# LRU gate products on 64 rows of TensorE, two at a time in two banks, with the second tile of outputs first

## The chip, the cores and the metric

The kernel runs on one core of one Trainium2 chip. The metric is the device time of one execution in microseconds (us). The kernel before takes 2714.79 us (median of 3 runs, 2714.78 to 2714.88).

## The reference

A decoder trunk of two layers on x of 1024 tokens by 1024 channels, in float32: layer 0 mixes tokens by retention, layer 1 by a Griffin block (below), each followed by a SwiGLU FFN, and one last norm. The change touches only the gates of the Griffin block, whose width is 1536 in 8 blocks of 192 channels:

```python
gate, u = jnp.split(h @ w_in, 2, axis=-1)
u = conv4(u) + conv_b
ub = u.reshape(B, S, LRU_BLOCKS, LRU_BLOCK_W)
r = sigmoid(einsum('bsnc,ncd->bsnd', ub, w_r) + b_r)
i = sigmoid(einsum('bsnc,ncd->bsnd', ub, w_i) + b_i)
log_a = (-LRU_C * softplus(-lam)) * r
a = exp(log_a)
b = sqrt(-expm1(2.0 * log_a)) * (i * u)
hs = scan(a, b)                      # hs[t] = a[t] * hs[t-1] + b[t]
y = hs * gelu(gate)
return y @ w_out
```

## The kernel before

**Products.** Each float32 matrix is kept as two fp32r parts, hi and lo. One product of a 128x128 weight tile with 512 tokens is three matmuls of TensorE, written by `three` (L745): hi by hi (L747), hi of the weights by lo (L750), lo of the weights by hi (L751). They add up in one bank of PSUM. PSUM has eight banks of 512 columns, and every output that a bank holds is an event: event e lies in bank e mod 8. TensorE raises the semaphore `psum_full` when an event is complete; the reader raises `psum_free` when it has used it. `free(e)` (L742) lets TensorE begin event e only when event e-8 and all before it have been read.

**Groups.** The 1536 channels are worked in four groups of 384, which is 2 blocks of 192 or 3 tiles of 128. Group g runs on TensorE in this order: `lru_into` for u (3 tiles), `lru_into` for the gelu gate (3 tiles), `lru_outof` (L1250) of the group before, then `lru_gates` (L1232). After the gates come the first tile of the next group's `lru_into`, which begins with `free` on its second event (L781), or in the last group four output blocks of the group before, each with a `free` of its own (L1282). Groups 0 and 3 are written out (L1257 to L1259, L1268 to L1290); groups 1 and 2 are a loop (L1260).

**The gates.** For each half of the tokens (hf) and each tile of outputs, r and i (m_i) are each one event. Blocks of 192 do not fall on tiles of 128. Outputs of tile 0 need input tiles 0 and 1, those of tile 1 need 0, 1 and 2, those of tile 2 need 1 and 2 (`MEETS`, L52). Of input tile 1 only rows 0 to 63 matter for output tile 0, and only rows 64 to 127 for output tile 2; the other 64 rows of those weight tiles (`wri_hi`, `wri_lo`) are zeros. A half of a group is 2 x (2 + 3 + 2) products, 42 matmuls, and a group 84.

**What the gates feed.** ScalarE (`gate_chain`, L1736) and VectorE (`gate_chain`, L2353) take items 0 to 5 in the order of the events: item i is tile i mod 3 of half i // 3. For one item ScalarE computes the sigmoid of r (L1743) and of i (L1748), then, two items together, tanh (L1757), exp (L1761) and sqrt (L1767), each behind a load of its table. VectorE multiplies u by i (L2361, `gated`; this raises `psum_free` by 2 for the item's two events), then L2369, L2373, the scan L2378 and the product with gelu (L2385). The order around the change, on ScalarE and on VectorE:

```python
gates(0); gates(1); tanh_exp((0, 1)); roots((0, 1)); gates(2); gates(3); y_round((0, 1))
gated((0, 1)); scans((0, 1), amid=lambda: gated((2,))); gated((3,)); y_split((0, 1)); gated((4, 5))
```

`amid` runs behind the first scan of a pair. L2390 (`y_split`) raises `y_ready`, for which `lru_outof` and the last output products (L1298) wait.

**u.** The conv writes `uc`; ScalarE rounds it to hi (L1733) and VectorE subtracts for lo (L2351, raises `u_ready`), in four pieces: tile 0, tile 1, and tile 2 in two halves. In groups 1 and 2 the hi and lo parts share their memory with those that `lru_outof` reads, so tile 2's pieces are made only when `lru_outof` is through. VectorE adds the outputs of `lru_outof` to the residual with L1952.

Of the kernel before, what the change touches and what calls it, by code (L numbers as in the profile page):

```python
# [14 lines left out]
P = 128  # L15
D = 1024
S = 1024
# [9 lines left out]
GT = 3  # L27
# [21 lines left out]

OT_AT = (0, SCORE_AT[3])  # L50

MEETS = [(0, 1), (0, 1, 2), (1, 2)]  # L52

U_PIECES = [(0, 0, S), (1, 0, S), (2, 0, BANK), (2, BANK, S)]

# [108 lines left out]
def build(nc, x, positions, mix_norm, ffn_norm, final_norm, ret_w_in, ret_w_out, lru_w_in, lru_conv_w,  # L164
# [3 lines left out]
    with ctx:  # L168
# [572 lines left out]
        def _(pe):  # L741
# [490 lines left out]
            def lru_gates(g, base, e0, u_hi, u_lo):  # L1232

                pe.wait_ge(wri_ready, 2 * g + 2)
                for hf in range(2):
                    for tile in range(GT):
                        for m_i in range(2):
                            e = e0 + (hf * GT + tile) * 2 + m_i
                            free(base + e)
                            if m_i == 0 and (hf, tile) in ((0, 0), (0, 1), (1, 1)):  # L1240

                                pe.wait_ge(u_ready, len(U_PIECES) * g + 2 + tile + hf)
                            for kt in MEETS[tile]:
                                w = slice(m_i * 1152 + kt * 384 + tile * P, m_i * 1152 + kt * 384 + (tile + 1) * P)
                                r = slice(kt * S + hf * 512, kt * S + (hf + 1) * 512)
                                m = three(bank(e), wri_hi[:, w], wri_lo[:, w], u_hi[:, r], u_lo[:, r],
                                          kt == MEETS[tile][0], kt == MEETS[tile][-1])
# [25 lines left out]
            for first in (0, 4):  # L1273
                for k in range(GT):
                    if first == 0:
                        pe.wait_ge(y_ready, (GROUPS - 2) * 6 + k + 4)
                        pe.wait_ge(w_ready, u0 + 12 + k + 1)
                    w = slice(k * 512, (k + 1) * 512)
                    for s in range(first, first + 4):
                        e = (L_OUT if first == 0 else L_OUT_LAST - 4) + s  # L1280
                        if k == 0:
                            free(base + e)  # L1282
                        c = k * S + s * P
                        m = three(bank(e), a_hi[:, c:c + P], a_lo[:, c:c + P], w_hi[:, w], w_lo[:, w],
                                  k == 0, k == GT - 1, s == (4 if k else 0))
                        if k == GT - 1:
                            m.then_inc(psum_full, 1)
                if first == 0:
                    lru_gates(GROUPS - 1, base, L_RI_LAST, h_hi, h_lo)
# [5 lines left out]

            def y_there(half, k, i):
                if i == 0:
                    pe.wait_ge(y_ready, (GROUPS - 1) * 6 + half * GT + k + 1)  # L1298
                if half == 0 and k == 0:

                    pe.wait_ge(psum_free, by_halves(3, 0, i) - 8 + 1)
# [9 lines left out]
        def _(act):  # L1311
# [424 lines left out]
            def gate_chain(g, base, e0, y_hi):  # L1736
                def gates(i):

                    tile = i % GT
                    if i >= 4:  # L1740
                        act.wait_ge(l_scan, 6 * g + i - 3)
                    full(base + e0 + 2 * i)
# [8 lines left out]
                def tanh_exp(items):  # L1751

                    for i in items:
                        if i >= 2:
                            act.wait_ge(l_scan, 6 * g + i - 1)
                        act.wait_ge(r_sig, 6 * g + i + 1)
                        nc.scalar.activation(s_buf[i % 2], r_buf[i % 4], ACT.Tanh,  # L1757
                                             scale=gc_gate[:, 21 + i % GT:22 + i % GT]).then_inc(r_tanh, 1)
                    for i in items:
                        act.wait_ge(r_tanh, 6 * g + i + 1)  # L1760
                        nc.scalar.activation(r_buf[i % 4], r_buf[i % 4], ACT.Exp,  # L1761
                                             scale=gc_gate[:, i % GT:i % GT + 1]).then_inc(a_exp, 1)

                def roots(items):

# [3 lines left out]
                def y_round(items):  # L1769
                    for i in items:  # L1770
                        act.wait_ge(y_out, 6 * g + i + 1)

                        act.wait_ge(psum_full, base + e0 + (6 if i < GT else 12))
                        at = i % GT * S + i // GT * 512
# [48 lines left out]
        def _(dve):  # L1823
# [528 lines left out]

            def gate_chain(g, y_hi, y_lo, meanwhile=lambda nh, blocks: None):  # L2353
                def cut(i):
                    return slice(i % GT * S + i // GT * 512, i % GT * S + i // GT * 512 + 512)

                def gated(items):

# [4 lines left out]
                def scans(items, between=lambda: None, amid=lambda: None):  # L2363
# [9 lines left out]
                        step.up(TT(uc[:, cut(i)], uc[:, cut(i)], s_buf[i % 2], ALU.mult))  # L2373
                    for j, i in enumerate(items):
                        dve.wait_ge(dve_step, first + j + 3)
                        tile, hf = i % GT, i // GT
# [121 lines left out]
```

## Time and profile before

| | before |
|---|---|
| median of 3 runs | 2714.79 us |
| the profiled execution's own time | 2714.54 us |
| its span | 2712.7 us |
| TensorE busy | 2673.3 us, 99% |
| VectorE busy | 1274.1 us, 47% |
| ScalarE busy | 826.6 us, 30% |
| GpSimd busy | 1259.5 us, 46% |
| mean granted TensorE clock | 0.998 |
| chain that ended last: TensorE, VectorE, ScalarE | 92%, 4%, 2% |

The span is the time from the first to the last instruction that the profiler saw; the time of an execution has 1.8 us more around it. Busy matmuls overlap each other, since a matmul's duration is counted to the end of its results. So the distance between the starts of two matmuls, and not their duration, is what one costs on TensorE.

### The profile page before, as it was taken

The numbers are of one execution on the slowest core, as the hardware profiler recorded it, in microseconds if no ns is written. First come the engines' busy times: TensorE is split into PE (matmuls) and PEld (weight loads), VectorE is DVE, ScalarE is ACT, GpSimd is POOL, SyncE is SP. The second block draws the span as 40 slices with busy tenths as digits, with TensorE's granted clock in tenths as the row PEclk, the third lists the DMA queues.
The fourth block names the chain that finished last, engine by engine and source line by source line (L and its number), as shares of the span: only waits on it lengthen the run. The fifth ranks groups of instructions, "written<-read, shape, count | busy, mean of one in ns | idle before, by whom it ended". The sixth has DMA issues, their size and how long they took to land.

```text
span 2712.7 us, 35233 instructions
## 1 busy us (share of the span) xinstructions
PE 2673.3 (99%) x12017; PEld 2212.2 (82%) x12017; DVE 1274.1 (47%) x1730; ACT 826.6 (30%) x1384; POOL 1259.5 (46%) x1204
## 2 busy tenths in 40 slices
PE   8999999999999999999999999999999999999998
PEld 6888888888888788888888788888877888888886
DVE  8333322323335854444444537365587444444445
ACT  3120120120124533333323524334355222222224
POOL 4324323323423466655555445363454556555553
PEclk9999999999999999999999999999999999999999
DMA  4101101101111111111211011111111111111212
GB/s 142 43 28 63 43 31 60 46 32 59 47 36 43 51 51 54 46 46 54 63 53 54 28 55 44 36 59 36 44 55 47 55 54 46 46 51 54 66 50 82
DMA packets 173624, 139.29 MB, mean 51 GB/s; under 512 B 9184, under 2 KB 143456, under 8 KB 173536
## 3 DMA queue, kind: packets, MB, share of 16 engines
q1 hardware_dynamic: 171440, 133.46, 15.8%
q10 hardware_dynamic: 2096, 4.62, 0.5%
q8 instruction: 59, 0.97, 0.1%
q14 instruction: 29, 0.24, 0.0%
HBM read 132.81 MB, written 5.24 MB: 51 GB/s over the span
## 4 chain that ended last, share of the span: by engine, by line
PE 92%; DVE 4%; ACT 2%; issue 1%; DMA 0%; POOL 0%; SPq 0%; DVEq 0%; ACTq 0%
PE ps L747 30%; PE ps L750 30%; PE ps L751 30%; DVE f_h_lo L2104 1%; PE ps L983 0%; ACT gate_buf L1318 0%; DVE residual L2289 0%; DVE residual L2451 0%; PE ps L823 0%; DVE h_sum_a L2093 0%; DVE gate_buf L2178 0%; DVE residual L1952 0%; DMA residual<-in_x 0%; ACT f_h_hi L1556 0%; DVE f_h_lo L2093 0%
## 5 line engine op out<-in xcount | busy, mean ns | idle before, releaser
L587 POOL TENSOR_TENSOR f_w_lo<-f_raw,f_w_hi 128x512 fp32r<-128x512 f32 x270 | 357.6, 1326 | 448.5 <-ACT f_w_hi L1507 366.0
L747 PE MATMUL ps<-f_h_hi,f_w_hi 128*128 128x512 f32 x1232 | 481.1, 391 | 4.9 <-DVE f_h_lo L2104 2.1
L751 PE MATMUL ps<-f_h_hi,f_w_lo 128*128 128x512 f32 x1232 | 479.5, 389 | 0.0
L750 PE MATMUL ps<-f_h_lo,f_w_hi 128*128 128x512 f32 x1232 | 479.4, 389 | 0.0
L545 POOL TENSOR_TENSOR small<-w_raw 128x1 f32<-128x1 f32 x200 | 59.9, 300 | 805.7 <-PE ps L747 796.1
L2289 DVE TENSOR_TENSOR residual<-ps,residual 128x512 f32<-128x512 f32 x352 | 239.3, 691 | 172.5 <-PE ps L751 172.5
L747 PEld LDWEIGHTS ps<-f_h_hi,f_w_hi 128*128 128x128 f32 x1232 | 231.2, 188 | 58.9 <-issue 4.3
L1507 ACT ACTIVATE f_w_hi<-f_raw 128x512 fp32r<-128x512 f32 x246 | 154.6, 629 | 384.0 <-PE ps L751 383.9
L751 PEld LDWEIGHTS ps<-f_h_hi,f_w_lo 128*128 128x128 f32 x1232 | 231.2, 188 | 48.3
L750 PEld LDWEIGHTS ps<-f_h_lo,f_w_hi 128*128 128x128 f32 x1232 | 231.3, 188 | 47.1
L747 PE MATMUL ps<-f_w_hi,f_act_hi 128*128 128x512 f32 x688 | 267.9, 389 | 0.6 <-POOL f_w_lo L587 0.6
L750 PE MATMUL ps<-f_w_lo,f_act_hi 128*128 128x512 f32 x688 | 267.6, 389 | 0.0
L751 PE MATMUL ps<-f_w_hi,f_act_lo 128*128 128x512 f32 x688 | 267.6, 389 | 0.0
L556 POOL TENSOR_TENSOR w_lo<-w_raw,w_hi 128x512 fp32r<-128x512 f32 x190 | 259.1, 1364 | 15.2
L747 PE MATMUL ps<-h_hi,w_hi 128*128 128x512 f32 x632 | 247.4, 392 | 0.1
L751 PE MATMUL ps<-h_hi,w_lo 128*128 128x512 f32 x632 | 246.0, 389 | 0.0
L750 PE MATMUL ps<-h_lo,w_hi 128*128 128x512 f32 x632 | 245.9, 389 | 0.0
L587 POOL TENSOR_TENSOR f_w_lo<-f_sum,f_w_hi 128x512 fp32r<-128x512 f32 x124 | 178.7, 1441 | 132.0 <-ACT f_w_hi L1507 124.6
L747 PE MATMUL ps<-w_hi,h_hi 128*128 128x512 f32 x528 | 205.7, 390 | 0.3 <-DVE gate_buf L1975 0.3
L751 PE MATMUL ps<-w_hi,h_lo 128*128 128x512 f32 x528 | 205.5, 389 | 0.0
L750 PE MATMUL ps<-w_lo,h_hi 128*128 128x512 f32 x528 | 205.5, 389 | 0.0
L2244 DVE TENSOR_TENSOR gate_buf<-ps,gate_buf 128x512 f32<-128x512 f32 x120 | 82.7, 689 | 235.2 <-PE ps L751 235.1
(302 smaller groups left out, 4630.3 us busy)
## 6 DMA issues: line engine op xcount, KB each, us to landing
f_raw<-in_ffn_w_gu SPq DMA_DIRECT2D x176, 256.0 KB, 3.3
w_raw<-in_ret_w_in SPq DMA_DIRECT2D x96, 256.0 KB, 2.7
f_raw<-in_ffn_w_down SPq DMA_DIRECT2D x88, 256.0 KB, 2.7
w_raw<-in_lru_w_in SPq DMA_DIRECT2D x48, 256.0 KB, 2.9
w_raw<-in_ret_w_out SPq DMA_DIRECT2D x32, 256.0 KB, 2.5
w_raw<-in_lru_w_out SPq DMA_DIRECT2D x24, 256.0 KB, 2.6
residual<-in_x SPq DMA_DIRECT2D x8, 512.0 KB, 7.1
out_y<-residual SPq DMA_DIRECT2D x8, 512.0 KB, 2.6
```

Source lines behind the costliest of these rows:

```text
L545: nc.gpsimd.tensor_tensor(small[:, 62:63], col, col, ALU.subtract)
L556: nc.gpsimd.tensor_tensor(lo, raw[:, cut], hi.bitcast(F32), ALU.subtract).then_inc(w_ready, 1)
L587: nc.gpsimd.tensor_tensor(lo, src, hi.bitcast(F32), ALU.subtract).then_inc(f_wready, 1)
L747: m = nc.tensor.matmul(o, l_hi, r_hi, start=start, stop=False, skip_group_check=onto)
L750: nc.tensor.matmul(o, l_hi, r_lo, start=False, stop=False, skip_group_check=onto)
L751: return nc.tensor.matmul(o, l_lo, r_hi, start=False, stop=stop, skip_group_check=onto)
L1507: nc.scalar.activation(f_unit(j, last)[0], src, ACT.Copy).then_inc(f_whi, 1)
L2104: TT(H_lo[:, h_cut(form, k)], src[:, t_cut(k)], H_hi[:, h_cut(form, k)].bitcast(F32), ALU.subtract).then_inc(hn_dve, 1)
L2244: TT(t, f_bank(u, p), t, ALU.add).then_inc(f_ev, 1)
L2289: TT(X[:, c], ps[:, b * BANK:(b + 1) * BANK], X[:, c], ALU.add).then_inc(f_ev, 1)
```

## The change

The gates' products are issued in another order, and those that meet only half of the rows are cut to these rows. For each half of the tokens TensorE now issues: output tile 0 by input tile 0 (r and i), output tile 1 by input tiles 0, 1 and 2, output tile 2 by input tile 2, and last (`halves_meet`) output tile 0 by rows 0 to 63 of input tile 1, alternating with output tile 2 by rows 64 to 127 of it. The two lie in two banks. Matmuls stay 42 per half: 30 of 128 rows and 12 of 64 rows. The events, and with them ScalarE's and VectorE's items, go by `GATE_TILES`: items 0 and 3 are tile 1, 1 and 4 tile 0, 2 and 5 tile 2. Items of tiles 0 and 2 are announced together, by one increment of 4 on the last matmul. The waits for `u_ready`, `psum_free` and `y_ready` move with that.

```diff
-MEETS = [(0, 1), (0, 1, 2), (1, 2)]
+GATE_TILES = (1, 0, 2)
...
                 for hf in range(2):
-                    for tile in range(GT):
+                    def event(tile, m_i):
+                        return e0 + (hf * GT + GATE_TILES.index(tile)) * 2 + m_i
+
+                    def operands(tile, m_i, kt, rows=slice(0, P)):
+                        w = slice(m_i * 1152 + kt * 384 + tile * P, m_i * 1152 + kt * 384 + (tile + 1) * P)
+                        r = slice(kt * S + hf * 512, kt * S + (hf + 1) * 512)
+                        return wri_hi[rows, w], wri_lo[rows, w], u_hi[rows, r], u_lo[rows, r]
+
+                    def meets(tile, kt, start, stop):
                         for m_i in range(2):
-                            e = e0 + (hf * GT + tile) * 2 + m_i
-                            free(base + e)
-                            if m_i == 0 and (hf, tile) in ((0, 0), (0, 1), (1, 1)):
-
-                                pe.wait_ge(u_ready, len(U_PIECES) * g + 2 + tile + hf)
-                            for kt in MEETS[tile]:
...
-                            m.then_inc(psum_full, 1)
+                            e = event(tile, m_i)
+                            if start:
+                                free(base + e)
+                            m = three(bank(e), *operands(tile, m_i, kt), start, stop)
+                            if stop:
+                                m.then_inc(psum_full, 1)
+
+                    def halves_meet():
+
+                        for m_i in range(2):
+                            a_w, a_wl, a_u, a_ul = operands(0, m_i, 1, slice(0, 64))
+                            b_w, b_wl, b_u, b_ul = operands(2, m_i, 1, slice(64, P))
+                            a, b = bank(event(0, m_i)), bank(event(2, m_i))
+                            nc.tensor.matmul(a, a_w, a_u, start=False, stop=False)
+                            nc.tensor.matmul(b, b_w, b_u, start=False, stop=False)
+                            nc.tensor.matmul(a, a_w, a_ul, start=False, stop=False)
+                            nc.tensor.matmul(b, b_w, b_ul, start=False, stop=False)
+                            nc.tensor.matmul(a, a_wl, a_u, start=False, stop=True)
+                            m = nc.tensor.matmul(b, b_wl, b_u, start=False, stop=True)
+
+                        m.then_inc(psum_full, 4)
+
+                    if hf == 0:
+                        pe.wait_ge(u_ready, len(U_PIECES) * g + 2)
+                    meets(0, 0, True, False)
+                    meets(1, 0, True, False)
+                    meets(1, 1, False, False)
+                    pe.wait_ge(u_ready, len(U_PIECES) * g + 3 + hf)
+                    meets(1, 2, False, True)
+                    meets(2, 2, True, False)
+                    halves_meet()
...
-                        pe.wait_ge(y_ready, g * 6 + k + 4)
+                        pe.wait_ge(y_ready, g * 6 + GATE_TILES.index(k) + 4)
...
-                    tile = i % GT
+                    tile = GATE_TILES[i % GT]
```

The other lines of the diff put `GATE_TILES` in the place of `i % GT` or of `k` wherever an item or an output product names its tile.

TensorE at the start of the gates of group 0 (`wri` are the gates' weights, `a` is u; the change shifts the line numbers, so L747 is now L749). Before:

```order
L747 MATMUL ps<-a_hi,wri_hi 128x512 [waits u_ready,psum_free,wri_ready]
L750 MATMUL ps<-a_lo,wri_hi 128x512
L751 MATMUL ps<-a_hi,wri_lo 128x512
L747 MATMUL ps<-a_hi,wri_hi 128x512
L750 MATMUL ps<-a_lo,wri_hi 128x512
L751 MATMUL ps<-a_hi,wri_lo 128x512
L747 MATMUL ps<-a_hi,wri_hi 128x512 [waits psum_free]
```

and now:

```order
L749 MATMUL ps<-a_hi,wri_hi 128x512 [waits psum_free,u_ready,wri_ready]
L752 MATMUL ps<-a_lo,wri_hi 128x512
L753 MATMUL ps<-a_hi,wri_lo 128x512
L749 MATMUL ps<-a_hi,wri_hi 128x512 [waits psum_free]
L752 MATMUL ps<-a_lo,wri_hi 128x512
L753 MATMUL ps<-a_hi,wri_lo 128x512
L749 MATMUL ps<-a_hi,wri_hi 128x512 [waits psum_free]
```

The first two events that TensorE opens are those of item 1 (tile 0), each with one product of three matmuls; item 0 (tile 1) is opened behind them. In order of issue the matmul that completes item 0's r is now the 21st and was the 6th, and item 1's r and i are complete with the 42nd and were with the 21st and the 30th.

TensorE at the end of the first half of the tokens, same group, before:

```order
L751 MATMUL ps<-a_hi,wri_lo 128x512
L747 MATMUL ps<-a_hi,wri_hi 128x512 [waits psum_free]
L750 MATMUL ps<-a_lo,wri_hi 128x512
L751 MATMUL ps<-a_hi,wri_lo 128x512
L747 MATMUL ps<-a_hi,wri_hi 128x512
```

and now:

```order
L753 MATMUL ps<-a_hi,wri_lo 128x512
L1261 MATMUL ps<-a_hi,wri_hi 128x512
L1262 MATMUL ps<-a_hi,wri_hi 128x512
L1263 MATMUL ps<-a_lo,wri_hi 128x512
L1264 MATMUL ps<-a_lo,wri_hi 128x512
L1265 MATMUL ps<-a_hi,wri_lo 128x512
L1266 MATMUL ps<-a_hi,wri_lo 128x512
L1261 MATMUL ps<-a_hi,wri_hi 128x512
```

L1261, L1263 and L1265 read rows 0 to 63, the other three rows 64 to 127; the six stand there twice, for r and for i.

TensorE from the last matmul of group 0's gates to the next group, now (before, the same rows stand there with their own lines, and the wait too):

```order
L1266 MATMUL ps<-a_hi,wri_lo 128x512
L1290 UNCONDITIONAL_BRANCH
L1290 ISA
L757 ISA [waits psum_free]
L749 MATMUL ps<-h_hi,w_hi 128x512 [waits w_ready]
L752 MATMUL ps<-h_lo,w_hi 128x512
```

The wait at L757 (L755 before) is `free` on the next group's second event, which is fulfilled when item 2 has been read by `gated`. Nothing moves there, and neither on ScalarE nor on VectorE: their rows are the same in number and order, with other tiles in them.

## Rows read from the trace of the kernel before

**Rows 1.** The page's part 1: busy time, share of the span and instructions
```profile
PE 2673.3 (99%) x12017; PEld 2212.2 (82%) x12017; DVE 1274.1 (47%) x1730; ACT 826.6 (30%) x1384; POOL 1259.5 (46%) x1204
```

**Rows 2.** Waits of TensorE, 1550 to 2100 us: total, times, longest us
```profile
PE ps L747 <- DVE a_lo L2351: 1.6, 2, 0.8
...
PE ps L747 <- DVE uc L2361: 0.2, 1, 0.2
```

**Rows 3.** Matmuls that read the gates' weights: count, ns min/median/max, starts
```profile
L747 PE MATMUL ps<-a_hi,wri_hi x84: 389/389/496, 1623.5 to 1878.0; 128*128 128x512 f32 x84
...
L747 PE MATMUL ps<-h_hi,wri_hi x28: 389/389/389, 1952.1 to 1970.5; 128*128 128x512 f32 x28
```

**Rows 4.** Timeline of TensorE, group 0's gates: start us, duration us, what
```profile
1623.53 0.39 PE L747 MATMUL ps<-a_hi,wri_hi 128*128 128x512 f32 x1
1623.53 0.19 PEld L750 LDWEIGHTS ps<-a_lo,wri_hi 128*128 128x128 f32 x1
1623.76 0.39 PE L750 MATMUL ps<-a_lo,wri_hi 128*128 128x512 f32 x1
...
1642.57 0.39 PE L747 MATMUL ps<-h_hi,w_hi 128*128 128x512 f32 x1
```

**Rows 5.** Timeline of ScalarE and VectorE, group 0
```profile
1630.53 0.69 ACT L1748 ACTIVATE xn<-ps,gc_gate 128x512 f32<-128x512 f32 x1 [1.35 <-PE ps L751]
...
1640.69 0.67 DVE L2361 TENSOR_TENSOR uc<-uc,xn 128x512 f32<-128x512 f32 x1
```

**Rows 6.** Chain of waits, 1950 to 1980 us (group 3): start us, us, what
```profile
1959.12 0.69 ACT xn L1748
...
1972.27 0.61 DVE uc L2361
1972.92 0.50 PE ps L747
```

**Rows 7.** Timeline, group 1's gates, of TensorE, ScalarE and VectorE
```profile
1740.49 0.39 PE L747 MATMUL ps<-a_hi,wri_hi 128*128 128x512 f32 x1
...
1744.15 0.50 PE L747 MATMUL ps<-a_hi,wri_hi 128*128 128x512 f32 x1 [0.78 <-DVE a_lo L2351]
...
1748.59 0.69 ACT L1748 ACTIVATE xn<-ps,gc_gate 128x512 f32<-128x512 f32 x1 [0.35 <-PE ps L751]
...
1758.75 0.66 DVE L2361 TENSOR_TENSOR uc<-uc,xn 128x512 f32<-128x512 f32 x1
...
1760.62 0.39 PE L747 MATMUL ps<-h_hi,w_hi 128*128 128x512 f32 x1
```

**Rows 8.** Timeline of TensorE: starts of gates 2 and 3, end of 2
```profile
1858.54 0.39 PE L747 MATMUL ps<-a_hi,wri_hi 128*128 128x512 f32 x1
...
1878.68 0.39 PE L747 MATMUL ps<-h_hi,w_hi 128*128 128x512 f32 x1
...
1952.12 0.39 PE L747 MATMUL ps<-h_hi,wri_hi 128*128 128x512 f32 x1
```

**Rows 9.** Timeline of VectorE: residual adds ahead of group 1's gates
```profile
1738.64 4.86 DVE L1952 TENSOR_TENSOR residual<-ps,residual 128x512 f32<-128x512 f32 x8
```

**Rows 10.** Timeline of weight loads in a run of matmuls of 128 columns
```profile
324.18 0.19 PEld L751 LDWEIGHTS ps<-a_hi,a_lo 128*128 128x128 f32 x1
...
324.29 0.19 PEld L747 LDWEIGHTS ps<-a_hi 128*128 128x128 f32 x1
```

**Rows 11.** TensorE's wait before layer 1, and windows (third number from the end: granted clock)
```profile
1548.42 5.09 PE L885 MATMUL ps<-ident,xn 128*128 128x128 f32 x24 [2.92 <-DVE xn L1849]
...
1545.00:1550.00 5.00, 2.00 (x8) 0.80 (x7) 3.66 (x9) 4.23 (x10) 0.00 (x0) 0.90 0.01 2
1550.00:1555.00 5.00, 5.00 (x29) 4.70 (x30) 3.97 (x8) 4.62 (x8) 1.10 (x2) 0.76 0.00 0
```

**Rows 12.** Timeline: last `y_split` on VectorE, and the output products that need it
```profile
2007.59 1.47 DVE L2390 TENSOR_TENSOR h_lo<-gate_buf,h_hi 128x512 fp32r<-128x512 f32 x2
...
2012.54 0.39 PE L747 MATMUL ps<-w_hi,h_hi 128*128 128x512 f32 x1
```

More of the change, by code:

```diff
@@ L1235, in lru_gates @@
                 for hf in range(2):
-                    for tile in range(GT):
-                        for m_i in range(2):
-                            e = e0 + (hf * GT + tile) * 2 + m_i
-                            free(base + e)
-                            if m_i == 0 and (hf, tile) in ((0, 0), (0, 1), (1, 1)):
-                                pe.wait_ge(u_ready, len(U_PIECES) * g + 2 + tile + hf)
-                            for kt in MEETS[tile]:
[L1244 to L1247, printed above, removed]
-                            m.then_inc(psum_full, 1)
+                    def event(tile, m_i):
+                        return e0 + (hf * GT + GATE_TILES.index(tile)) * 2 + m_i
@@ L1275, in _ @@
                     if first == 0:
-                        pe.wait_ge(y_ready, (GROUPS - 2) * 6 + k + 4)
+                        pe.wait_ge(y_ready, (GROUPS - 2) * 6 + GATE_TILES.index(k) + 4)
                         pe.wait_ge(w_ready, u0 + 12 + k + 1)
@@ L1297, in y_there @@
                 if i == 0:
-                    pe.wait_ge(y_ready, (GROUPS - 1) * 6 + half * GT + k + 1)
+                    pe.wait_ge(y_ready, (GROUPS - 1) * 6 + half * GT + GATE_TILES.index(k) + 1)
                 if half == 0 and k == 0:
@@ L1757, in tanh_exp @@
                         nc.scalar.activation(s_buf[i % 2], r_buf[i % 4], ACT.Tanh,
-                                             scale=gc_gate[:, 21 + i % GT:22 + i % GT]).then_inc(r_tanh, 1)
+                                             scale=gc_gate[:, 21 + GATE_TILES[i % GT]:22 + GATE_TILES[i % GT]])\
+                            .then_inc(r_tanh, 1)
                     for i in items:
@@ L1761, in tanh_exp @@
                         nc.scalar.activation(r_buf[i % 4], r_buf[i % 4], ACT.Exp,
-                                             scale=gc_gate[:, i % GT:i % GT + 1]).then_inc(a_exp, 1)
+                                             scale=gc_gate[:, GATE_TILES[i % GT]:GATE_TILES[i % GT] + 1])\
+                            .then_inc(a_exp, 1)
                 def roots(items):
@@ L1773, in y_round @@
                         act.wait_ge(psum_full, base + e0 + (6 if i < GT else 12))
-                        at = i % GT * S + i // GT * 512
+                        at = GATE_TILES[i % GT] * S + i // GT * 512
                         nc.scalar.activation(y_hi[:, at:at + 512], R3[:, at:at + 512], ACT.Copy)\
@@ L2354, in cut @@
                 def cut(i):
-                    return slice(i % GT * S + i // GT * 512, i % GT * S + i // GT * 512 + 512)
+                    at = GATE_TILES[i % GT] * S + i // GT * 512
+                    return slice(at, at + 512)
                 def gated(items):
@@ L2375, in scans @@
                         dve.wait_ge(dve_step, first + j + 3)
-                        tile, hf = i % GT, i // GT
+                        tile, hf = GATE_TILES[i % GT], i // GT
                         start = uc[:, tile * S + 511:tile * S + 512] if hf else 0.0
```

## The prediction

> **What bounds the kernel now.** I read the page's busy shares first: TensorE is busy for 2673.3 of 2712.7 us, 99%, and no other engine for half of the span [rows 1]. So a microsecond of TensorE's work counts if nothing else keeps TensorE waiting at that place, and a wait put in front of TensorE counts in full. Next, the waits of TensorE in layer 1 [rows 2]. Two belong to the change. One is for u's lo part (L2351), twice 0.8 us. The other is for `gated` (L2361), 0.2 us: short, but it tells that the gate chain of ScalarE and VectorE is already level with TensorE at one place. That is what decides here.
>
> The cost of a matmul is the distance of starts. 4 x 84 matmuls read the gates' weights (84 + 28 of each of the three forms) [rows 3]. Group 0's 84 take from 1623.53 to 1642.57 us, when the next group's first one starts: 19.04 us, or 0.2267 us each, which I call a slot. A matmul lasts 0.39 us until its results are there, 0.16 us longer than its slot, and the weights of the next are loaded meanwhile, in 0.19 us [rows 4].
>
> **The chain behind the gates.** I count from T0, the start of a group's first gate matmul. In group 0 the sigmoid of item 1's i starts at T0 + 7.00 (1630.53), 0.04 us behind the result of the 30th matmul (T0 + 29 slots + 0.39 = T0 + 6.96). Item 2 has been read at 1640.69 + 0.67 = 1641.36, T0 + 17.83 [rows 5]. That is 10.83 us from the one to the other. The distance repeats where I look: 1748.59 to 1759.41 in group 1 [rows 7]. It holds tanh, exp and sqrt of two items with their table loads, and four operations and a scan of VectorE, all in a row; their order does not change. In group 0 the next group can begin at T0 + 17.9 and TensorE comes at T0 + 19.04: the chain has 1.1 us to spare. In group 3 it has none: the chain of waits runs from the sigmoid at 1959.12 (T0 + 7.00 again, T0 being 1952.12 [rows 8]) to `gated` of item 3 and from there into the matmul at 1972.92 [rows 6].
>
> **1. Item 1 is complete later.** It was complete with the 30th matmul, r long before i; now both come with the last of the first half. If two half-row matmuls share a slot, that is the last of 30 + 6 slots: its result is there at T0 + 35 slots + 0.39 = T0 + 8.32. The second of a pair needs its own load; where loads follow each other as closely as they can, their starts are 0.11 us apart [rows 10], so I add 0.11. Sigmoid of r at T0 + 8.48; the one of i, which waited alone before, comes some 0.58 us behind it (a ScalarE operation of this size, 0.69 us less the overlap of 0.11), at T0 + 9.06. The chain is 2.06 us later, plus what the entry into 64-row matmuls costs, d.
>
> **2. The entry, d.** No row shows a change from 128 to 64 rows. Below: 0, the load hides as in every row. A gain is excluded, since the half-row matmuls move the same 512 columns and two loads fill 0.22 of a 0.227 us slot. Above: the results before must be out (0.16 us) and the load is bare (0.19 us), 0.35 us [rows 4]. I take 0.2, between the ends but nearer the bare drain. The Trainium skill, "TensorEngine Tiling (Array Packing)", Key Properties, says that a change of tiling mode drains TensorE; no run here shows it yet, and by it d would lie between 0.16 and 0.35, which leaves the result as it is.
>
> **3. The next start of TensorE, group by group.** Item 2 read at T0 + 17.83 + 2.06 + d = T0 + 19.89 + d; the matmul follows 0.05 us later [rows 6], and a restart costs 0.15 us in the matmuls behind it. This is from group 1: its 84 take 20.13 us, of which the wait itself is 0.94 (1744.15 against T0 + 12 slots = 1743.21) and 0.15 the rest [rows 7]. So T0 + 20.1 + d in every group.
> - Group 0: 19.04 before, so +1.06 + d.
> - Groups 1 and 2: 20.13 and 20.14 before [rows 7, 8], since they waited for tile 2's u after 12 matmuls. Now this wait stands behind 18 matmuls, T0 + 4.08, and u was there at T0 + 3.6: it vanishes. The new place comes out the same: -0.03 and -0.04, + d each.
> - Group 3: behind its gates four output blocks begin, the third of which needs item 3. It began at T0 + 20.80 [rows 6, 8] and now 2.06 + d later.
>
> **4. Earlier events at the start.** TensorE now opens item 1's events first, which lie two banks further. In groups 1 and 2 this asks that the third residual add be through: adds start 0.6 us apart from 1738.64, so it ends at 1740.52, against T0 = 1740.49 [rows 9, 7]. With the restart 0.2 us in each, 0.4.
>
> **5. What TensorE saves.** Twelve slots a group, 48 x 0.2267 = 10.9 us, and the 2.2 us of the u waits. It is ready for the next group at T0 + 16.3, plus up to 1.4 us for going into and out of 64 rows twice, so at T0 + 17.7 at the latest, and waits until T0 + 20.3. All of it becomes waiting, and the second half's entry is hidden there too. The cover is the chain; without it, TensorE's time would count.
>
> **6. Other waits.** `y_ready` of the last group is given at 2009.06 and the products that need its items start at 2012.54 [rows 12]; both shift with TensorE. Nothing in the work of the DMA queues, ScalarE or VectorE is added.
>
> Sum: 1.06 - 0.03 - 0.04 + 2.06 + 0.4 + 4 x 0.2 = 4.25 us; 3.45 with d = 0 and 4.85 with d = 0.35. Against the profiled execution's 2714.54 this gives 2718.8; the median of the runs is 0.25 higher, so 2719.0.
>
> The Trainium skill ("Trainium Kernel Development and Optimization", Best Practices) warns of this change as such: tiling TensorE speeds up the products but not what empties PSUM. The group 3 wait agrees (0.2 us for `gated` already). Counted by TensorE alone, the sum would be the gain of rival C below.
>
> **Rivals.** A measurement of this kernel can tell about 0.2%, 5.4 us, from no change.
> - **A, the forecast**: pairs share slots, the chain sets the next start. 2718.2 to 2719.6. Chance 0.62; in 0.05 of it an unseen cost lifts it above the bound, as more than 0.5 us of d a group would.
> - **B, slower: the half-row matmuls do not run side by side.** Place: `halves_meet` of the first half. The change then only reorders. Each pair takes two slots, the chain starts 6 slots - 0.11 = 1.25 us later in each of four groups, +5.0: 2724.0. It decides from the point where a pair takes over 0.28 us (0.05 us more for each of the 24 pairs on the chain is 1.2 us). For it: nothing in the trace has ever run two matmuls at once, and loads need 0.11 us each, so that a pair's two loads just fit in a slot. Against: the two have different rows and banks, and the load rate does suffice. 0.15. The Trainium skill ("TensorE: Matmul & The Clock Gate", Part 3) says that matmuls on different row groups overlap; no row here shows it, and by it B would be out.
> - **D, slower: TensorE's clock falls in the new waits.** TensorE would now stand still for some 2.6 us in each group (its last result at T0 + 16.5 + 0.2 for the seconds of the pairs + 4 x 0.2 = T0 + 17.5, the restart at T0 + 20.1 + d). The trace has one wait of that size in full swing: 2.92 us at 1545.5, followed by short transposes. The granted clock is then 0.90 and 0.76 over two windows of 5 us, part of the time at 1.2 instead of 2.4 GHz: (0.10 + 0.24) x 5 = 1.7 us lost [rows 11]. Against: those transposes leave TensorE's array mostly unused, here full matmuls follow at once. Two falls give +3.4: 2722.4; one 2720.7, four 2725.8. Chance 0.18.
> - **C, faster: TensorE's own work counts**, because the chain is shorter than I read. Minus 10.9, minus 2.2, plus 8 x 0.4 for entries and exits: -9.9, 2704.9. Against it stand the 10.83 us that repeat and the wait for `gated` that is there now. 0.05.
>
> **The numbers.** A is the likeliest, so 2719.0. Within 0.2% lies most of A: 0.57. Slower: B, D and the rest of A, 0.15 + 0.18 + 0.05 = 0.38. Faster: C, 0.05. The range begins a little under A's lower end, 2717.4, for steps of the chain that I may have counted 0.2 us too long in each group, and reaches over one or two falls of the clock to B with d = 0.3, 2724.4. It leaves out C and the worst of D.
>
> **What will show it.** In the changed kernel the sigmoid of item 1's i should start about 9.3 us behind the first gate matmul, and be followed by `gated` of item 2 after 10.8 us. TensorE should show three or four new waits for `gated`, some 2 to 3 us each, and none for tile 2's u; starts from first gate matmul to next group 20.3 us in groups 0 to 2. In `halves_meet` the starts of the two matmuls of a pair should lie 0.11 us or less apart and pairs 0.23 us; 0.23 us from each to the next is B. A granted clock under 1.00 behind the gates is D. I am wrong in the main if TensorE does not wait for `gated`, or if item 2's release moves by another amount than item 1.

## The result, and the profile after

The change takes 2724.08 us (median of 6 runs, 2723.8 to 2725.94) against 2714.89 for the kernel before on the same chip (6 runs, 2714.78 to 2717.12): ratio 1.0034, 95% interval 1.0024 to 1.0044. It is slower by 9.2 us, 0.34%, which is beyond the 0.2% that the prediction took for no change. The forecast was 2719.0; the time lies at the upper end of the range. What lies between is rival D, not with one or two falls of the clock but with all four.

The page's part 1 of the changed kernel, against [rows 1]:

```profile
PE 2672.5 (98%) x12017; PEld 2206.3 (81%) x12017; DVE 1277.0 (47%) x1730; ACT 826.0 (30%) x1384; POOL 1258.4 (46%) x1204
```

TensorE's busy time moves by 0.8 us, although 48 slots of 0.227 us are gone: this line shows neither what was saved nor what was lost. The loss is in the waits of TensorE, 1550 to 2100 us (total, times, longest):

```profile
PE ps L749 <- DVE uc L2394: 12.1, 5, 3.0
```

It was 0.2 us in one wait [rows 2], and the row for u's lo part is gone. Timeline of TensorE, the pairs of group 0's first half:

```profile
1630.54 0.39 PE L753 MATMUL ps<-a_hi,wri_lo 128*128 128x512 f32 x1
1630.86 0.49 PE L1261 MATMUL ps<-a_hi,wri_hi 64*128 64x512 f32 x1
1630.86 0.49 PE L1262 MATMUL ps<-a_hi,wri_hi 64*128 64x512 f32 x1
1631.19 0.39 PE L1263 MATMUL ps<-a_lo,wri_hi 64*128 64x512 f32 x1
1631.20 0.39 PE L1264 MATMUL ps<-a_lo,wri_hi 64*128 64x512 f32 x1
...
1632.45 0.50 PE L749 MATMUL ps<-a_hi,wri_hi 128*128 128x512 f32 x1
1632.79 0.40 PE L752 MATMUL ps<-a_lo,wri_hi 128*128 128x512 f32 x1
```

The two of a pair start together and take one slot. Going in costs 0.09 us (0.32 from 1630.54 to 1630.86, against 0.23) and 0.10 in the next distance; coming out costs about as much again. From 1630.54 to 1632.79, eight distances of starts, it is 2.25 us in place of 1.81, so once in and once out costs 0.44. The chain behind it, timelines of ScalarE, VectorE and TensorE in group 0, whose T0 is now 1623.97:

```profile
1633.15 0.68 ACT L1778 ACTIVATE xn<-ps,gc_gate 128x512 f32<-128x512 f32 x1
...
1643.30 0.67 DVE L2394 TENSOR_TENSOR uc<-uc,xn 128x512 f32<-128x512 f32 x1
...
1644.10 0.49 PE L749 MATMUL ps<-h_hi,w_hi 128*128 128x512 f32 x1 [2.97 <-DVE uc L2394]
```

Item 1's i is at T0 + 9.18 (T0 + 7.00 before, [rows 5]), item 2 has been read 10.82 us later (10.83), and the next group starts at T0 + 20.13 (19.04, [rows 4]) behind a wait of 2.97 us. The other groups, same timeline, of each T0 and the next start, and in group 3 the third output block too:

```profile
1743.82 0.50 PE L749 MATMUL ps<-a_hi,wri_hi 128*128 128x512 f32 x1
...
1764.10 0.49 PE L749 MATMUL ps<-h_hi,w_hi 128*128 128x512 f32 x1 [2.97 <-DVE uc L2394]
...
1863.81 0.50 PE L749 MATMUL ps<-a_hi,wri_hi 128*128 128x512 f32 x1
...
1884.03 0.69 PE L749 MATMUL ps<-h_hi,w_hi 128*128 128x512 f32 x1 [2.89 <-DVE uc L2394]
...
1959.21 0.39 PE L749 MATMUL ps<-h_hi,wri_hi 128*128 128x512 f32 x1
...
1979.26 0.50 PE L749 MATMUL ps<-w_hi,a_hi 128*128 128x512 f32 x1 [2.89 <-DVE uc L2394]
...
1982.18 0.79 PE L749 MATMUL ps<-w_hi,a_hi 128*128 128x512 f32 x1 [0.39 <-DVE uc L2394]
```

Behind each of the four waits stand matmuls of another speed. Timeline behind the first, and windows around the first three (the number before the last two is the granted clock):

```profile
1645.43 0.63 PE L753 MATMUL ps<-h_hi,w_lo 128*128 128x512 f32 x1
1645.85 0.63 PE L749 MATMUL ps<-h_hi,w_hi 128*128 128x512 f32 x1
...
1648.41 0.51 PE L749 MATMUL ps<-h_hi,w_hi 128*128 128x512 f32 x1
```

```profile
1640.00:1645.00 5.00, 2.03 (x14) 1.34 (x11) 5.00 (x7) 3.87 (x6) 0.27 (x1) 1.00 0.00 0
1645.00:1650.00 5.00, 5.00 (x17) 3.96 (x16) 4.63 (x8) 4.29 (x8) 4.92 (x3) 0.66 0.00 0
1760.00:1765.00 5.00, 2.03 (x13) 1.32 (x10) 5.00 (x7) 3.87 (x6) 0.27 (x1) 0.97 0.00 0
1765.00:1770.00 5.00, 5.00 (x17) 3.97 (x16) 4.63 (x8) 4.29 (x8) 4.92 (x3) 0.69 0.00 0
1880.00:1885.00 5.00, 2.11 (x13) 1.35 (x12) 5.00 (x7) 3.88 (x6) 0.13 (x1) 0.92 0.02 3
1885.00:1890.00 5.00, 5.00 (x18) 4.00 (x17) 4.63 (x8) 4.27 (x8) 4.92 (x3) 0.74 0.00 0
```

For some 3 us a matmul costs 0.42 us in place of 0.227: 1.2 GHz in place of 2.4. Each pair of windows lacks 0.34 x 5 = 1.7 us. From the next group's start to the following T0 it is 99.72, 99.71 and 75.18 us, where it was 97.92, 97.92 and 73.44.

The account, up to the start of layer 1's FFN, where both kernels wait for the same add (before, then after):

```profile
2034.58 0.50 PE L747 MATMUL ps<-f_h_hi,f_w_hi 128*128 128x512 f32 x1 [1.48 <-DVE residual L1952]
```

```profile
2044.26 0.50 PE L749 MATMUL ps<-f_h_hi,f_w_hi 128*128 128x512 f32 x1 [1.45 <-DVE residual L1984]
```

That is 9.68 us: 0.44 was there at T0 of group 0; the starts behind the gates give 1.09 + 0.15 + 0.08 + 2.17 = 3.49; the stretches between them 1.80 + 1.79 + 1.74; the last one, 1982.18 to 2044.26 against 1972.92 to 2034.58, 0.42.

### The profile page after: what moved, and what is told of

Its sections match the earlier page's. It is cut to its first block, busy times and chain, and to the rows that moved or that the text cites. A ratio compares the mean times of both kernels' runs of the same rounds, so it can differ in the third digit from the quotient of the medians.

```text
span 2722.4 us, 35229 instructions
## 1 busy us (share of the span) xinstructions
PE 2672.5 (98%) x12017; PEld 2206.3 (81%) x12017; DVE 1277.0 (47%) x1730; ACT 826.0 (30%) x1384; POOL 1258.4 (46%) x1204
## 4 chain that ended last, share of the span: by engine, by line
PE 92%; DVE 4%; ACT 3%; issue 1%; DMA 0%; POOL 0%; SPq 0%; DVEq 0%; ACTq 0%
PE ps L749 30%; PE ps L753 30%; PE ps L752 30%; DVE f_h_lo L2136 1%; PE ps L985 0%; ACT gate_buf L1348 0%; DVE residual L2321 0%; DVE residual L2484 0%; PE ps L825 0%; DVE h_sum_a L2125 0%; PE ps L887 0%; DVE gate_buf L2210 0%; DMA residual<-in_x 0%; ACT f_h_hi L1586 0%; DVE f_h_lo L2125 0%
## 5 line engine op out<-in xcount | busy, mean ns | idle before, releaser
L749 PE MATMUL ps<-f_h_hi,f_w_hi 128*128 128x512 f32 x1232 | 481.1, 391 | 4.8 <-DVE f_h_lo L2136 2.1
L547 POOL TENSOR_TENSOR small<-w_raw 128x1 f32<-128x1 f32 x200 | 51.8, 259 | 816.0 <-PE ps L749 806.1
L749 PEld LDWEIGHTS ps<-f_h_hi,f_w_hi 128*128 128x128 f32 x1232 | 231.2, 188 | 59.0 <-issue 4.4
L749 PE MATMUL ps<-f_w_hi,f_act_hi 128*128 128x512 f32 x688 | 267.9, 389 | 0.6 <-POOL f_w_lo L589 0.6
L749 PE MATMUL ps<-h_hi,w_hi 128*128 128x512 f32 x632 | 249.9, 395 | 8.8 <-DVE uc L2394 8.8
L749 PE MATMUL ps<-w_hi,h_hi 128*128 128x512 f32 x528 | 205.7, 390 | 0.3 <-DVE gate_buf L2007 0.3
```

The costliest lines, as they stand in the source:

```text
L547: nc.gpsimd.tensor_tensor(small[:, 62:63], col, col, ALU.subtract)
L749: m = nc.tensor.matmul(o, l_hi, r_hi, start=start, stop=False, skip_group_check=onto)
```

## The experiments

Each ran beside the kernel before on the same chip, in 5 rounds. That one's medians there were 2715.46 us for experiments 1, 2, 4 and 5, 2715.08 for 6, 7 and 10, and 2714.79 for 3, 8 and 9. The change itself did not run again beside them, so differences to it of less than 1 us say nothing. In the expectations T1 is the account above (the chain and the clock), called the first theory here; T2 and T3 are rivals to it. Falls and waits are read from one execution of each kernel, the profiled one.

**1. Are the half rows what counts?** The change with all 128 rows in the pairs, so that nothing can run side by side:

```diff
-a_w, a_wl, a_u, a_ul = operands(0, m_i, 1, slice(0, 64))
-b_w, b_wl, b_u, b_ul = operands(2, m_i, 1, slice(64, P))
+a_w, a_wl, a_u, a_ul = operands(0, m_i, 1)
+b_w, b_wl, b_u, b_ul = operands(2, m_i, 1)
```

> The change with its order, but the 12 half-row matmuls of each half read all 128 rows (the other 64 rows of those weights are zeros), so nothing can share a slot. Chain theory (T1: the next start is set by the release of item 2, and the clock falls because TensorE stands still for 3 us): item 1's sigmoid of i starts at T0 + 10.3 instead of 9.2, the next group at T0 + 21.3; TensorE is ready at T0 + 19.04 and stands for about 2.1 us. If that is too short for the clock to fall, 2722.7 us, a little below the change though it has 48 slots more on TensorE; if it falls in all four, 2728.5. Rival T2 (the fall of the clock comes from the 64-row matmuls, not from standing still): granted clock 1.00 behind the gates, 2722.7. Rival T3 (pairs cost or save something on the path): the time would differ from the change by the 10.9 us of the 48 slots, 2735.

Measured: 2725.36 us, ratio 1.0035 (1.0021 to 1.0049). It lies between the two times of the first theory. In the profiled execution, the slowest of the five (2727.78 us), the clock fell behind two of the four waits and not behind the others; the other four took 2724.77 to 2725.38 us at a mean granted clock of 0.997 and 0.998 in place of 0.996, so they had fewer falls. Timeline of TensorE, three of the starts:

```profile
1645.87 0.49 PE L749 MATMUL ps<-h_hi,w_hi 128*128 128x512 f32 x1 [2.06 <-DVE uc L2394]
...
1767.01 0.49 PE L749 MATMUL ps<-h_hi,w_hi 128*128 128x512 f32 x1 [2.05 <-DVE uc L2394]
...
1981.17 0.50 PE L749 MATMUL ps<-w_hi,a_hi 128*128 128x512 f32 x1 [1.98 <-DVE uc L2394]
```

and the windows behind these three:

```profile
1645.00:1650.00 5.00, 4.13 (x13) 3.32 (x14) 4.88 (x9) 3.18 (x7) 3.49 (x2) 0.74 0.00 0
...
1770.00:1775.00 5.00, 5.00 (x24) 4.14 (x23) 3.36 (x4) 4.97 (x8) 4.84 (x5) 1.00 0.07 17
...
1980.00:1985.00 5.00, 3.27 (x8) 2.16 (x9) 5.00 (x8) 3.18 (x6) 0.00 (x0) 0.69 0.00 0
1985.00:1990.00 5.00, 5.00 (x16) 3.88 (x16) 1.63 (x3) 4.97 (x8) 2.04 (x3) 0.63 0.00 0
```

48 slots more of TensorE's work, 10.9 us, cost 1.3 us by the medians, and 0.7 when each kernel is compared with its own runs of the kernel before. In the profiled executions the stretch from T0 of group 0 to the FFN's first matmul is 423.22 us, against 420.29: the first halves' pairs make the chain later by 1.1 us in each group, 4.5 together, and the clock takes 1.5 less. The second halves' 24 slots end in the wait and cost nothing. Behind waits of the same 2.0 us the clock fell or did not, so executions can differ in this; behind the last one it stayed low for twice as long.

**2. The same waits, filled.** The change with 12 matmuls by weights that are zeros (added onto a sum that is still open, so nothing changes in it) ahead of the pairs of each group's second half:

```diff
                     meets(2, 2, True, False)
+                    if hf == 1:
+                        for _ in range(4):
+                            z, r = slice(256, 384), slice(512, 1024)
+                            three(bank(event(2, 0)), wri_hi[:, z], wri_lo[:, z], u_hi[:, r], u_lo[:, r], False, False)
                     halves_meet()
```

> The change, with 12 more matmuls of 128 rows (zero weights, 2.7 us) per group ahead of the second half's pairs, so that TensorE works where it stood still. T1: the chain is untouched, the next group starts at T0 + 20.1 as in the change, TensorE stands 0.3 us instead of 3.0 there, the granted clock stays at 1.00, and the kernel gets about 5.8 us faster than the change, 2718.3, by 48 matmuls more. T2 (64-row matmuls lower the clock): 2724, as the change, clock still falls. If TensorE's own work counted: 2724 + 10.9 = 2735.

Measured: 2718.95 us, ratio 1.0014 (1.0005 to 1.0023), 5.1 us under the change. Waits of TensorE:

```profile
PE ps L749 <- DVE uc L2398: 2.1, 5, 1.3
```

The next groups start at T0 + 20.13, 20.29, 20.23 and 20.06, as in the change, and the granted clock is 1.00 in every window around them. More work on the busiest engine made the kernel faster than the change is.

**3. Half the fill** (`range(2)` in place of `range(4)`), to see a length in between.

> e2_fill_wait with 6 in place of 12 fill matmuls a group: the waits for `gated` should be 1.36 us longer than there, 1.5 to 1.6 us in groups 0 to 3, and the starts of the next groups the same, T0 + 20.1 to 20.3. The question is TensorE's clock: behind waits of 3.0 us it fell in four of four, behind 2.0 us in two of four, behind 1.3 us in none. If it falls behind none, the time is that of e2_fill_wait, 2719 us; each fall adds about 1.45 to 1.8 us; four would give 2725.

Measured: 2719.16 us, ratio 1.0015 (1.0006 to 1.0024). Waits of TensorE, and windows behind the first two:

```profile
PE ps L749 <- DVE uc L2398: 7.5, 5, 1.6
```

```profile
1645.00:1650.00 5.00, 5.00 (x24) 4.13 (x23) 4.64 (x8) 3.84 (x7) 4.74 (x3) 1.00 0.01 3
...
1765.00:1770.00 5.00, 5.00 (x24) 4.13 (x23) 4.22 (x6) 4.98 (x9) 4.92 (x4) 1.00 0.00 0
```

The same chain, the same starts, 5.4 us more waiting than in 2, and the time of 2. So waiting itself costs nothing here while the clock stays, and the 64-row matmuls by themselves do not lower it; the whole 4.9 us to the change are the falls. They can be read piece by piece: from a group's end to the next T0 this kernel takes 98.10, 98.15 and 73.58 us. The change takes 1.62, 1.56 and 1.60 more, and 0.46 more at the end: 5.2 together in the profiled executions.

**4. Sooner for item 1.** `GATE_TILES` (0, 1, 2) again, pairs kept: tile 0 by input 0, the pairs (which open tile 2's banks), tile 1, then tile 2 by input 2. `meets` and `halves_meet` take m_i here, and each event is announced by itself:

```diff
-                    meets(0, 0, True, False)
-                    meets(1, 0, True, False)
-                    meets(1, 1, False, False)
-                    pe.wait_ge(u_ready, len(U_PIECES) * g + 3 + hf)
-                    meets(1, 2, False, True)
-                    meets(2, 2, True, False)
-                    halves_meet()
+                    for m_i in range(2):
+                        meets(0, m_i, 0, True, False)
+                    for m_i in range(2):
+                        halves_meet(m_i)
+                    for m_i in range(2):
+                        meets(1, m_i, 0, True, False)
+                        meets(1, m_i, 1, False, False)
+                        if m_i == 0:
+                            pe.wait_ge(u_ready, len(U_PIECES) * g + 3 + hf)
+                        meets(1, m_i, 2, False, True)
+                    for m_i in range(2):
+                        meets(2, m_i, 2, False, True)
```

> The pairs without the new order: items are tiles 0, 1, 2 as before; TensorE issues tile 0 by input 0, then the pairs (tile 2 is opened by them), then tile 1, then tile 2 by input 2. Item 0 complete at 12 matmuls and item 1 at 30, as before, plus 0.32 us for going into and out of 64 rows. T1: item 1's sigmoid of i at T0 + 7.3, next start at T0 + 18.35 in group 0 (19.04 before), 1.3 us sooner than before in groups 1 and 2 (tile 2's u is no longer waited for, but 0.5 us for a residual add is), 0.3 us later in group 3; TensorE stands for 1.3 us and the clock stays at 1.00: 2711.8. T2 (64-row matmuls lower the clock): 4 x 1.45 us more, 2717.6, with a granted clock under 1.00 behind the gates. If TensorE's own work counted: 2705.

Measured: 2712.15 us, ratio 0.9988 (0.9979 to 0.9997), as the first theory had it. Starts at T0 + 18.42, 18.59, 18.50 and 18.34, behind waits of 1.0 to 1.2 us, no fall. It is 3.3 us under the kernel before. The two waits for u that are gone (1.09 us each with their restarts) make up 2.2 of it; what the pairs alone bring in this order no run shows.

**5. Item 2 released from the chain.** The change, with item 2's sigmoids ahead of tanh on ScalarE (`gates(2)` before `tanh_exp((0, 1))`) and on VectorE `gated((0, 1, 2))` in place of `amid`.

> The change, with ScalarE's sigmoids of item 2 and VectorE's product with them moved ahead of tanh of items 0 and 1, so that item 2's banks are read some 9 us sooner. T1: TensorE no longer waits for item 2 in groups 0 to 2 and begins the next group at T0 + 17.0 with a clock of 1.00; the chain of items 0 to 5 ends about 0.6 us later than in the change, so a wait of about 1.4 us for the conv of the next group appears instead before its second gate tile; in group 3 item 3 is read at T0 + 23.5, TensorE stands 5 us there and the clock falls once. Sum about +0.6 us against before: 2715.4, between 2713 and 2718. If the release of item 2 does not set the next start: 2724, as the change.

Measured: 2729.07 us, ratio 1.0051 (1.0038 to 1.0065). Missed by 13.7 us. Timelines of TensorE, VectorE and GpSimd:

```profile
1640.65 0.50 PE L749 MATMUL ps<-h_hi,w_hi 128*128 128x512 f32 x1
...
1642.94 1.62 POOL L558 TENSOR_TENSOR w_lo<-w_raw,w_hi 128x512 fp32r<-128x512 f32 x1
1643.33 2.31 DVE L2411 TENSOR_TENSOR_SCAN uc<-tmp,uc 128x512 f32<-128x512 f32 x1
...
1688.12 0.49 PE L749 MATMUL ps<-h_hi,w_hi 128*128 128x512 f32 x1 [3.66 <-DVE uc L2368]
...
1986.13 0.79 PE L749 MATMUL ps<-w_hi,a_hi 128*128 128x512 f32 x1 [4.79 <-DVE uc L2394]
```

The first step came true: the next group starts at T0 + 17.09, with no wait. But the same chain has a second end, the next group's conv, for which TensorE now stands still for 3.66 us at 1688.12 (1.4 reckoned). ScalarE's two operations moved into it make it 1.1 us longer. And TensorE, 3 us earlier, gives GpSimd its weights 3 us earlier: GpSimd's first operation behind the gates starts at 1641.29 and not at 1644.73, and VectorE's scan beside it takes 2.31 us, 1.22 in the change. The granted clock fell behind all four of its long waits (3.66, 3.66, 3.46 and 4.79 us): it is 0.86, 0.73, 0.86 and 0.87 over the 11 or 12 us from each restart.

**6. Sooner for item 1, and nothing longer.** Experiment 4 with `GATE_TILES` (0, 2, 1): tiles 0 and 2, which share the pairs, are items 0 and 1, and tile 1, which shares nothing, is item 2.

```diff
-                    for m_i in range(2):
-                        meets(1, m_i, 0, True, False)
-                        meets(1, m_i, 1, False, False)
-                        if m_i == 0:
-                            pe.wait_ge(u_ready, len(U_PIECES) * g + 3 + hf)
-                        meets(1, m_i, 2, False, True)
+                    meets(1, 0, 0, True, False)
+                    pe.wait_ge(u_ready, len(U_PIECES) * g + 3 + hf)
                     for m_i in range(2):
                         meets(2, m_i, 2, False, True)
+                    meets(1, 1, 0, True, False)
+                    for m_i in range(2):
+                        meets(1, m_i, 1, False, False)
+                        meets(1, m_i, 2, False, True)
```

> The half-row pairs are kept, but the items go in the order tile 0, tile 2, tile 1: TensorE issues tile 0 by input 0, the pairs, three matmuls of tile 1, tile 2 by input 2, then the rest of tile 1. T1 (the chain behind item 1 sets the next start only as long as it is longer than TensorE's own work): item 1 is complete with the 21st slot, about T0 + 5.2 us, so the sigmoid of its i starts at about T0 + 5.3 and item 2 has been read at T0 + 16.2. TensorE itself needs 72 slots and the entries and exits, about 17.1 us, so it is the bound and waits for `gated` nowhere: next starts T0 + 17.1 to 17.3 in all groups, third block of group 3 at about T0 + 18.9, no fall of the clock. Against the kernel before: -1.9 - 2.9 - 2.9 - 1.9 = -9.6, so about 2705.5 to 2706 us. T2 (the chain's length is not what it was, because what ends it is something else, such as ScalarE or VectorE being held up by other work at that time): item 2's release does not follow item 1 by 10.8 us, the waits for `gated` stay, 2710 or more. Rival T3: TensorE gets ahead of the next group's conv or of the weights that GpSimd prepares, new waits there of 1 us or more a group: 2709 or more.

Measured: 2708.52 us, ratio 0.9976 (0.9966 to 0.9986), 2.5 to 3 us over what was expected. In groups 0 and 3 TensorE is at T0 + 17.22 without a wait, as expected; in groups 1 and 2 it waits 1.2 and 1.1 us, and the third output block of group 3 waits 0.6 us for item 3. Timelines of VectorE, ScalarE and TensorE, group 1 (T0 is 1739.54):

```profile
1743.87 0.17 DVE L2429 TENSOR_SCALAR gc_gate<-gc_gate 128x3 f32<-128x3 f32 x1
1744.13 1.28 ACT L1774 ACT_TABLE_LOAD   x1 [3.16 <-DVE gc_gate L2429]
...
1747.15 0.70 ACT L1779 ACTIVATE xn<-ps,gc_gate 128x512 f32<-128x512 f32 x1
...
1757.33 0.67 DVE L2395 TENSOR_TENSOR uc<-uc,xn 128x512 f32<-128x512 f32 x1
```

Item 1's products are there, but ScalarE waits for the gates' scales and biases, which VectorE copies behind its adds and u's lo parts. Again 10.85 us from item 1's i to the end of item 2: the chain is as long, its start is held by something else.

**7. The order alone**: experiment 6 with all 128 rows in the pairs, as in 1.

> e5_tile1_last with all 128 rows in the pairs' matmuls (the other rows of the weights are zeros, so the result is the same): the order alone, without the packing. T1: TensorE's own 84 slots are the bound in every group, next start T0 + 19.04, third block of group 3 at T0 + 20.7; item 1 complete at the 27th slot, item 2 read at about T0 + 17.4, no wait for `gated`, none for tile 2's u. Against the kernel before: 0 - 1.1 - 1.1 - 0.1 = -2.3, about 2713. The difference to e5_tile1_last is then what the packing brings when TensorE is the bound: 48 slots less 8 entries and exits, 10.9 - 2.6 = 8.3 us at most, 7.5 expected. T2: nearly no difference between the two, as there was between the change and its full-row version.

Measured: 2712.41 us, ratio 0.999 (0.9981 to 0.9999). All four groups take 19.04 us (1624.01 to 1643.05, 1740.97 to 1760.01) with no wait for `gated` or u. So the same packing that was worth 1.3 us in the change is worth 3.9 to experiment 6, where 7.5 were expected. Experiment 8, which also has the scales and biases earlier, is 6.3 under this one, each against its own runs of the kernel before; experiment 8 with full rows was not run.

**8. The scales and biases earlier**: experiment 6 with the two operations at L2427 to L2429 moved behind `gelu_seen`, ahead of the adds.

> e5_tile1_last with the copy of the gates' scales and biases (two small operations of VectorE, for which ScalarE's first sigmoid of a group waits) moved from behind the residual adds and u's lo parts to in front of them. The trace of e5_tile1_last shows in groups 1 and 2 that ScalarE starts on the gates 4.6 us behind T0, when VectorE has made these columns, and so has item 1's i at T0 + 7.6 in place of T0 + 5.5; item 2 is read 10.85 us later and TensorE waits 1.2 and 1.1 us. T1 (item 1's i sets the start of the chain, whatever holds it up): with the columns there in time ScalarE's table load runs at once behind its roundings of u, item 1's i comes at about T0 + 5.5 and TensorE's waits in groups 1 and 2 go: next starts T0 + 17.2 in place of 18.6 and 18.5, -2.7 us: about 2706. Group 3's wait of 0.6 stays. Rival: ScalarE's own roundings or VectorE's u parts set it, then the waits stay over 0.8 us and the time at 2708 or more.

Measured: 2705.84 us, ratio 0.9967 (0.9955 to 0.9979). Group 1, ScalarE and TensorE (T0 is 1739.20):

```profile
1740.65 1.28 ACT L1774 ACT_TABLE_LOAD   x1
...
1744.63 0.69 ACT L1779 ACTIVATE xn<-ps,gc_gate 128x512 f32<-128x512 f32 x1
...
1756.45 0.39 PE L749 MATMUL ps<-h_hi,w_hi 128*128 128x512 f32 x1
```

T0 + 5.43 for item 1's i, T0 + 17.25 for the next start, no wait.

**9. And item 3**: experiment 8 with `amid=lambda: gated((2, 3))` and `gated((3,))` gone.

> e8_gate_columns_early, and VectorE multiplies item 3 right behind item 2, behind the first scan, in place of behind the second scan and two products. Only group 3 can gain: its third output block waits 0.6 us for item 3 and restarts for 0.15, -0.75 us, about 2705.3. Against it: the second scan and all behind it are 0.6 us later until item 3's old place, and the same from there on, so nothing else should move.

Measured: 2705.38 us, ratio 0.9966 (0.9954 to 0.9978), 9.4 us below the kernel before and the best of all. No wait for `gated` is left; the difference to 8 is no larger than the runs' own spread.

**10. Must the pairs alternate?** Experiment 6 with the three matmuls of rows 0 to 63 issued first and the three of rows 64 to 127 behind them.

> e5_tile1_last with the six half-row matmuls in the order three of rows 0 to 63, then three of rows 64 to 127, in place of alternating. If two matmuls run side by side only when they stand next to each other and have different rows, each run of 12 has 3 such neighbours in place of 6 pairs: 3 slots more in each of 8 runs, 5.4 us: about 2711. If TensorE lets the later three overtake (queues by row half), the same time as e5_tile1_last, 2705.5 to 2706. If the overlap needs the same operands' form in both, nothing overlaps: 6 slots more in each of 8, 10.9 us less the entries: about 2716.

Measured: 2708.95 us, ratio 0.9977 (0.9968 to 0.9986), the time of experiment 6. Timeline of TensorE; in the program L1259, L1260, L1261 stand ahead of L1262:

```profile
1625.22 0.49 PE L1259 MATMUL ps<-a_hi,wri_hi 64*128 64x512 f32 x1
1625.23 0.49 PE L1262 MATMUL ps<-a_hi,wri_hi 64*128 64x512 f32 x1
1625.56 0.39 PE L1260 MATMUL ps<-a_lo,wri_hi 64*128 64x512 f32 x1
1625.57 0.39 PE L1263 MATMUL ps<-a_lo,wri_hi 64*128 64x512 f32 x1
```

The fourth starts with the first. The Trainium skill ("TensorE: Matmul & The Clock Gate", Part 3, The mechanism) speaks of a reorder window, by which weight loads for other rows go ahead of matmuls in flight, and says that the matmuls themselves keep their order. Here page and measurement differ: L1262 starts at 1625.23, 0.33 us before L1260, which stands ahead of it.

## Why the prediction was right, and where it was wrong

The chain of steps held, the clock did not. Without the falls the time is 2719.2 us (experiment 3); the forecast was 2719.0. From T0 of group 0 to the FFN's first matmul experiment 3 takes 3.9 us more than the kernel before, where 4.25 were forecast.

- **What bounds** (the chain is level with TensorE): right. 10.8 us from item 1's i to item 2 read stand in every kernel here that keeps the chain's order, wherever its start is moved to (experiments 4, 6, 8).
- **Step 1**, item 1 later: T0 + 9.26 with d, measured 9.18. The offset of 0.11 us inside a pair does not exist.
- **Step 2**, d = 0.2: 0.09 + 0.10, right; coming out costs the same. It lies ahead of the second half, where the wait takes it up.
- **Step 3**, next starts: 20.3 us forecast; 20.13, 20.28, 20.22 and 20.05 measured. The sum of the shifts was 3.85 with d, measured 3.49; each group is 0 to 0.25 us under the forecast.
- **Step 4**, T0 later in groups 1 and 2: 0.4 reckoned for the two, 0.18 and 0.23 measured in experiment 3, and 0.14 in group 3, not reckoned.
- **Step 5**, the savings become waiting: right. TensorE waited 2.9 to 3.0 us and not 2.6 (under D): its last result was there at T0 + 17.2 and not 17.5, and the 2.6 left out the d that the restart at T0 + 20.1 + d has.
- **Rival B** is out: pairs share their slots. **Rival C** is out too, for the chain is as long as it was read. But its 9.9 us are nearly what the pairs and the better order give when TensorE no longer waits for the chain: 9.0 and 9.4 us in experiments 8 and 9.
- **Rival D** is what happened, and here the prediction failed. Its price of 1.7 us a fall was nearly right: 1.6 by the distances, 1.7 by the windows. Its chance, 0.18, and its count, one or two, were not. I named one wait of 2.92 us with a fall behind it as evidence, and then set against it that "here full matmuls follow at once". No row showed that what follows a wait undoes the standing still in it. Four waits as long as the only known one, all behind the same dense work, were likelier to go one way than to be four throws (at 2.0 us, in experiment 1, they did not go one way). With the waits of step 5 at 2.6 to 3 us, D with all four should have been the likeliest: 2725.8 by its own sum, 2724.1 measured. The sum is 1.7 high, mostly by the fourth fall: it costs only 0.46 us, because nearly all of it (1979.88 to 1982.77) lies ahead of the third output block, which waits for item 3 anyway.
- **The range** held by luck. It left out "the worst of D", which is what came, and its upper end was taken from B, which did not come. Had the fourth fall cost 1.6 us like the others, the time would have been about 2725.2, outside.

What stays open is what makes the clock fall. It did behind all four waits of 2.9 to 3.0 us in the change and two of four of 2.0 us in experiment 1, and behind none of 1.6 us or less in the gates (experiments 2, 3, 4, 6). Which of the waits of 2.0 us it takes was not settled. Nor does the length of the wait alone decide it: in layer 0 of the profiled execution of experiment 2 it fell behind waits of 0.98 and 0.78 us, with four short transposes between them and twelve behind. Windows there:

```profile
830.00:835.00 5.00, 3.23 (x17) 2.40 (x16) 4.55 (x7) 0.84 (x3) 4.84 (x7) 0.96 0.14 52
835.00:840.00 5.00, 5.00 (x21) 4.36 (x21) 2.95 (x5) 1.79 (x3) 4.76 (x8) 0.70 0.55 175
```

The same fall stands in that of experiment 9, and none in those of experiment 8 and of the change, whose windows are at 1.00 there behind the same two waits. So the same place can go either way from one execution to the next; only the profiled executions can tell, and each kernel has one.

## What to carry to other kernels

Before work is taken off the busiest engine, find what that engine will wait for next, and ask whether the new order makes that come later: here the two tiles that share the pairs had to be read first, and the change issued the pairs last, behind the whole of the third tile. A wait opened in front of TensorE is priced twice, by its length and by the clock behind it, and if it is as long as one that already shows a fall, count a fall for every place (here four of four at 2.9 to 3.0 us). When a chain decides, move its start and leave its length: experiments 4 and 8, which did this, met their numbers; 6 and 10 missed theirs by some 3 us, since the start was held elsewhere in two groups; and 5, which added work to the chain, lost by its other end.

## What was not expected of the hardware

- Two matmuls on different halves of the rows start within 0.01 us of each other and take one slot of 0.227 us, and three issued later overtake to do so (experiment 10). Going in and out costs 0.44 us for six pairs: 2.25 us from the last full matmul ahead of them to the second behind (1630.54 to 1632.79), against 8 x 0.227 = 1.81.
- A fall of the clock lasts about 3 us and costs 1.6; behind a wait of 1.98 us in experiment 1 it lasted twice as long (0.69 and 0.63 over two windows of 5 us).
- VectorE's scan of 512 columns took 1.22 us alone and 2.31 us beside GpSimd's subtraction (experiment 5, against the same scan in the change, with GpSimd idle). So a TensorE that starts earlier can make the chain behind it longer.
